# Turning gathered token tiles with VectorE's 32x32 transposes and sixteen small transfers in a routed-expert stage

## Chip, cores and metric

One core of a Trainium2 chip. The metric is the device time of one execution in microseconds; the program runs the whole layer once. Everything is float32.

## What is computed

One layer of a streaming encoder for 1024 tokens of width 1024: a gated DeltaNet branch and a sliding-window attention branch, added to the residual, and then a mixture of experts. Only the last part matters here:

```python
def hier_moe(h, ...):
    # top-1 of 4 groups, then top-2 of the 4 experts in it -> gates (tokens x 16)
    y = jnp.zeros_like(tok)
    for e in range(N_EXPERTS):                      # 16
        gu = tok @ w_gate_up[e]                     # 1024 -> 512
        act = jax.nn.silu(gu[:, :256]) * gu[:, 256:]
        y = y + gates[:, e:e + 1] * (act @ w_down[e])   # 256 -> 1024
```

`tok` is the RMS-normalised token row times `ffn_norm_g`, the gain that the kernel applies after it has turned the rows.

## The kernel before, in words

The front of the kernel (eight tiles of 128 tokens, 0 to about 660 us) writes the normalised rows to `h_mid` in HBM and the residual to `out`. Routing then gives each expert a list of token rows. An expert has one full tile of up to 128 rows, and up to two half tiles of 64 rows for what is over; a half tile that is empty is skipped by a branch on TensorE, which puts one small 64x64 transpose in its place (`nothing`, L827), while the other engines do their part for it always. Whatever doesn't fit goes through a spill loop.

The stage is a software pipeline over i = 0..15 (`ORDER` maps i to an expert), each engine with its own hand-written order:

- GpSimd gathers: `gather(i)` brings full tile i from `h_mid` into one of three buffers `hg[i % 3]`, `gather_half` the half tiles, `gather_base` the present rows of `out`; `scatter` writes the sum back. In iteration i it issues `gather(i + 3)` behind the gathers of the bases, and waits there until tile i has been turned.
- SyncE loads the weights, 2 MB (`load_gate_up`, L358) and 1 MB (`load_down`, L364) per expert, into a ring of four, so up to three experts ahead.
- TensorE, iteration i: `gate_up(i)` (8 steps of 128 rows, listed as 16 matmuls), `turn_glu(i-1)`, `turn_half_glu(i-1)`, `turn_halves(i)`, `down(i-1, 0)`, `down_half(i-1, 1)`, `gate_up_halves(i)`, `turn_rows(i+1)`, `down(i-1, 1)`, `down_half(i-1, 0)`. `turn_rows` is eight 128x128 transposes of the gathered rows into banks pm0 and pm1. The two halves of `down` use one bank, pm4, so the second waits until VectorE has added the first out (`y_ready`).
- VectorE, iteration i: `copy_half(i, 0/1)` (L1891), `add_out(i-1, 0)` (L1918), `add_half(i-1, 1)` (L1925), `copy_rows(i+1)` (L1825: two operations that copy the turned rows from PSUM to `hgT` times the gain), `add_out(i-1, 1)`, `add_half(i-1, 0)`, `swiglu(i)` (L1900, L1902), `half_swiglu(i, 0/1)` (L1909, L1911).
- ScalarE, iteration i: `gate_tanh(i)` (L1223), `copy_glu(i-1)` (L1229), `copy_half_glu(i-1, 0/1)` (L1236), `half_tanh(i, 0/1)` (L1243). It starts no transfer in this stage.

`gate_up(i+1)` needs `hgT`, which has one buffer: `copy_rows(i+1)` waits for `gate_up(i)` to end. `down(i-1, 0)` needs `copy_glu(i-1)`, which stands behind `gate_tanh(i)` in ScalarE's order. Matmuls and most transposes show as L423 and L426, the lines of the helpers `mm` and `turn`.

Of the kernel before, what the change touches and what calls it, by code (L numbers as in the profile page):

```python
# [70 lines left out]
def build(nc, x, x_turned, attn_norm_g, w_in, conv_w, a_log, dt_bias, out_norm_g, q_norm_g, k_norm_g, sinks,  # L71
          w_out, ffn_norm_g, b_group, b_expert, w_router, w_gate_up, w_down, out, dbg=None):
    with ExitStack() as ctx:
# [141 lines left out]
        hgT = flat(ctmp)[:, 0:D].rearrange("p (k n) -> p k n", n=P)  # L215
        hgT_half = [flat(ci)[:, c * 512:c * 512 + 512].rearrange("p (k n) -> p k n", n=P) for c in range(2)]
# [50 lines left out]
        M = sems("turned hT_ready gu_done tanh_ready glu_step glu_ready glu_turned glu_copied down_done y_ready", "slots_")  # L267
# [14 lines left out]
        def gated(i, c=0):  # L282

            return 3 * i + (3, 1, 2)[c] if i == NE - 1 else nth(i, c)

# [135 lines left out]
        def _(pe):  # L421
# [464 lines left out]
            def turn_glu(i):  # L886
                pe.wait_ge(M.glu_ready, gated(i))
# [22 lines left out]
            def turn_half_glu(i):  # L910
                pe.wait_ge(M.glu_ready, gated(i, 2))
                if_filled_both(i, pm[6:8], lambda c: None, lambda c: turn(pm[6 + c][:, 2 * P:3 * P], glu_half[c]), M.glu_turned)
# [82 lines left out]
        def _(act):  # L995
# [223 lines left out]
            def gate_tanh(i):  # L1219
                act.wait_ge(M.gu_done, gated(i))  # L1220
                if i:
                    act.wait_ge(M.glu_ready, gated(i - 1))
                act.activation(tnh, pm[2 + i % 2][:, 0:DE], ACT.Tanh, scale=0.5).then_inc(M.tanh_ready, 1)  # L1223

# [14 lines left out]
            def half_tanh(i, c):  # L1239
                act.wait_ge(M.gu_done, gated(i, c + 1))  # L1240
                if i:
                    act.wait_ge(M.glu_ready, gated(i - 1, c + 1))
# [3 lines left out]
            spilled = act.value_load(full[0:1, 0:1], min_val=0, max_val=2 ** (NE + 1) - 1)  # L1246
            for i in range(NE):
# [6 lines left out]
                for c in range(2):  # L1254
                    half_tanh(i, c)
            gate_tanh(NE - 1)
# [10 lines left out]
        def _(v):  # L1267
# [552 lines left out]
            def copy_rows(i):  # L1820
                v.wait_ge(M.turned, nth(i))
# [65 lines left out]
            def copy_half(i, c):  # L1887
                v.wait_ge(M.turned, nth(i, c + 1))
# [5 lines left out]

            def swiglu(i):
# [4 lines left out]
                v.scalar_tensor_tensor(tnh, tnh, 1.0, bank[:, 0:DE], ALU.add, ALU.mult).then_inc(M.glu_step, 1)  # L1900
                v.wait_ge(M.glu_step, gated(i))
                v.scalar_tensor_tensor(glu, tnh, 0.5, bank[:, DE:2 * DE], ALU.mult, ALU.mult).then_inc(M.glu_ready, 1)  # L1902

            def half_swiglu(i, c):
# [4 lines left out]
                v.scalar_tensor_tensor(t, t, 1.0, pm[6 + c][:, 0:P], ALU.add, ALU.mult).then_inc(M.glu_step, 1)  # L1909
                v.wait_ge(M.glu_step, gated(i, c + 1))  # L1910
# [17 lines left out]
            spilled = v.value_load(full[0:1, 0:1], min_val=0, max_val=2 ** (NE + 1) - 1)  # L1928
            for i in range(NE - 1):
# [10 lines left out]
                copy_rows(i + 1)  # L1940
# [5 lines left out]
                half_swiglu(i, 1)  # L1946
            last = NE - 1
# [23 lines left out]
        def _(g):  # L1971
# [123 lines left out]
            def gather(i):  # L2095
                if i >= IN:
                    g.wait_ge(gathered[i % IN], 16 * uses(i - IN, IN))
                    g.wait_ge(M.turned, nth(i - IN))
# [3 lines left out]
            def gather_half(i, c):  # L2102
                u = 2 * i + c
                if u >= HIN:
                    g.wait_ge(half_gathered[u % HIN], 16 * uses(u - HIN, HIN))
                    g.wait_ge(M.turned, nth(i - HIN // 2, c + 1))
# [44 lines left out]
            for i in range(NE + 1):  # L2151
                if i < NE:
# [3 lines left out]
                if i + IN < NE:  # L2156
                    gather(i + IN)
# [52 lines left out]
```

## Time and profile before

| | us |
|---|---|
| median of 3 runs | 948.48 (947.60 to 948.57) |
| the profiled execution | 949.3 |
| its span, first to last instruction | 947.5 |
| TensorE / VectorE / ScalarE / GpSimd busy | 900.2 / 586.8 / 230.7 / 217.4 |
| transfers over the span | 113.9 MB, 120 GB/s on average |

The page divides the span into forty slices of 23.7 us; a digit is the busy share in tenths, and PEclk the clock that TensorE was granted. The chain of work is followed back from the last instruction. In the lists in order of time a row gives the start, the time taken, engine, line, operation, output<-inputs, shape and count, and in brackets how long the engine had been idle before and what released it. Several operations of one kind that follow each other are merged into one row. "ACTq" and "SPq" are the instructions with which ScalarE and SyncE start transfers; they do not count as busy.

### The profile page before, as it was taken

To read this page: it belongs to the slowest core of one execution; us is meant where nothing else is said; L and a number is where in the kernel's file an instruction comes from. 1 tells how busy PE (TensorE), PEld (TensorE's weight loads), DVE (VectorE), ACT (ScalarE), POOL (GpSimd) and SP (SyncE) were. 2 spreads that over 40 slices of the span, in tenths; PEclk is the share of its full clock that TensorE was granted. 3 is DMA by queue.
4 is the path that set the end of the run, shared out by engine and by line. 5 is a ranking of instruction groups with operands and counts; after the bars stand their busy time and mean duration, and the time that the engine had idled before them with its cause. 6 is when DMAs were issued, how large, how long until landed. Compare 5 with 4: busy or idle time off the path is not lost.

```text
span 947.5 us, 16439 instructions
## 1 busy us (share of the span) xinstructions
PE 900.2 (95%) x6268; PEld 603.3 (64%) x6268; DVE 586.8 (62%) x1746; ACT 230.7 (24%) x637; POOL 217.4 (23%) x302
## 2 busy tenths in 40 slices
PE   5999899999999999999999999889899999999986
PEld 5687687696596787768769656565544554544532
DVE  2367776785785786687687577768344433544443
ACT  1343331431432332342243134123001001011000
POOL 7020020020020001002002000300444544555653
PEclk9999999999999999999999999999999999999998
DMA  8920101010010010110100004704559869899521
GB/s 307 395 112 1 45 24 45 15 55 23 24 67 12 35 68 1 46 46 23 46 23 2 29 18 144 278 24 142 178 163 338 282 212 313 292 324 345 183 87 43
DMA packets 50475, 113.86 MB, mean 120 GB/s; under 512 B 11207, under 2 KB 12487, under 8 KB 50384
## 3 DMA queue, kind: packets, MB, share of 16 engines
q1 hardware_dynamic: 34064, 87.07, 25.7%
q0 software_dynamic: 14592, 25.22, 7.8%
q8 instruction: 62, 1.02, 0.5%
q10 hardware_dynamic: 1728, 0.31, 0.2%
q14 instruction: 29, 0.24, 0.1%
HBM read 112.54 MB, written 25.17 MB: 145 GB/s over the span
## 4 chain that ended last, share of the span: by engine, by line
PE 86%; DVE 7%; DMA 2%; SPq 2%; issue 1%; POOL 0%; ACT 0%; POOLq 0%; DVEq 0%
PE pm L423 78%; PE pm L426 7%; DMA w_sb<-in_w_in 2%; DVE pqkv L1491 1%; SPq L351 1%; PE pm L827 1%; SPq L334 1%; DMA qkvT<-h_mid,w_sb 1%; DVE xT L1314 0%; DVE X L1673 0%; DVE bs L1735 0%; DVE ctmp L1825 0%; DVE sc L1659 0%; DVE aTm L1686 0%; DVE pT L1556 0%
## 5 line engine op out<-in xcount | busy, mean ns | idle before, releaser
L423 PEld LDWEIGHTS pm<-hT,w_sb 128*128 128x128 f32 x1544 | 176.4, 194 | 5.5 <-issue 2.9
L423 PE MATMUL pm<-hT,w_sb 128*128 128x128 f32 x1544 | 177.5, 277 | 1.9 <-DVE hT L1443 1.9
L423 PE MATMUL pm<-w_sb,hT 128*128 128x512 f32 (+1 forms) x384 | 153.4, 542 | 0.6 <-DMA w_sb<-in_w_in 0.6
L2030 POOL TENSOR_TENSOR tail<-tail,rows 128x512 f32<-128x512 f32 x8 | 10.8, 1346 | 485.9 <-ACT aTm L1046 485.9
L423 PE MATMUL pm<-wo_sb,pT 128*128 128x512 f32 x256 | 115.4, 597 | 2.7 <-ACT pT L1093 1.4
L423 PE MATMUL pm<-w_sb,ctmp 128*128 128x512 f32 (+1 forms) x264 | 102.7, 600 | 2.1 <-DVE ctmp L1825 2.1
L423 PEld LDWEIGHTS pm<-w_sb,hT 128*128 128x128 f32 x384 | 69.9, 193 | 52.2 <-issue 46.6
L1491 DVE SCALAR_TENSOR_TENSOR pqkv<-ci,cw,pqkv 128x128 f32<-128x128 f32 x288 | 77.4, 344 | 15.8 <-ACT pqkv L1025 15.6
L423 PEld LDWEIGHTS pm<-wo_sb,pT 128*128 128x128 f32 x256 | 46.6, 190 | 52.8 <-issue 48.8
L423 PEld LDWEIGHTS pm<-w_sb,ctmp 128*128 128x128 f32 (+1 forms) x264 | 39.9, 175 | 58.9 <-issue 58.5
L1891 DVE TENSOR_TENSOR ci<-pm,gain 128x512 f32<-128x512 f32 x32 | 20.6, 685 | 77.1 <-PE pm L426 38.7
L1673 DVE TENSOR_TENSOR X<-X,pm 128x256 f32<-128x256 f32 (+1 forms) x40 | 16.7, 418 | 54.3 <-PE pm L423 54.3
L423 PE MATMUL pm<-w_sb,Y 128*128 128x512 f32 x96 | 48.0, 623 | 2.4 <-issue 2.4
L1223 ACT ACTIVATE X<-pm 128x256 f32<-128x256 f32 x16 | 6.1, 384 | 163.3 <-PE pm L423 163.3
L1825 DVE TENSOR_TENSOR ctmp<-pm,gain 128x512 f32<-128x512 f32 x32 | 20.5, 683 | 31.3 <-PE pm L426 31.3
L2127 POOL DMA_INDIRECT pqkv<-out,w_sb x24 | 24.1, 1005 | 61.9 <-DMA out<-pqkv,w_sb 55.0
L423 PEld LDWEIGHTS pm<-X,aTm 64*64 64x64 f32 x640 | 23.2, 138 | 22.0 <-DVE X L1673 14.2
L423 PE MATMUL pm<-X,aTm 64*64 64x64 f32 x640 | 27.8, 227 | 8.0 <-DVE X L1673 6.9
L1012 ACT ACTIVATE ci<-pm 128x512 f32<-128x512 f32 x22 | 13.2, 601 | 90.2 <-PE pm L423 75.6
L1134 ACT ACTIVATE Y<-pm 128x256 f32<-128x256 f32 (+1 forms) x48 | 18.4, 384 | 68.6 <-PE pm L423 68.6
L1020 ACT ACTIVATE tail<-pm 128x512 f32<-128x512 f32 (+1 forms) x24 | 12.7, 528 | 88.4 <-PE pm L423 88.4
L1542 DVE TENSOR_TENSOR sc<-sc,pm 128x512 f32<-128x512 f32 x16 | 11.0, 685 | 36.7 <-PE pm L423 36.5
(340 smaller groups left out, 1456.6 us busy)
## 6 DMA issues: line engine op xcount, KB each, us to landing
w_sb<-in_w_gate_up SPq DMA_DIRECT2D x12, 2048.0 KB, 14.7
w_sb<-in_w_down SPq DMA_DIRECT2D x12, 1024.0 KB, 6.3
wo_sb<-in_w_gate_up SPq DMA_DIRECT2D x4, 2048.0 KB, 13.5
w_sb<-in_w_in SPq DMA_DIRECT2D x3, 2048.0 KB, 20.5
xt<-in_x SPq DMA_DIRECT2D x8, 512.0 KB, 4.3
xT<-in_x_turned SPq DMA_DIRECT2D x8, 512.0 KB, 3.6
w_sb<-in_w_in SPq DMA_DIRECT2D x4, 1024.0 KB, 13.4
wo_sb<-in_w_out SPq DMA_DIRECT2D x1, 4096.0 KB, 21.9
```

The source lines that it names most:

```text
L423: return pe.matmul(o_, lhsT=l_, rhs=r_, start=start, stop=stop, skip_group_check=True)
L426: return pe.transpose(o_, in_, ident[:, :])
L1012: ins = act.activation(ci[:, H * c:H * c + H, HALO:HALO + P], heads(pm[BANK[c]]), ACT.Copy)
L1020: act.activation(tail[:, c0 - 3 * HP:c0 - 3 * HP + n], pm[BANK[c]][:, 0:n], ACT.Copy).then_inc(F.chunk_copied, 1)
L1134: act.activation(Yd[rows_], heads(pm[3], CH)[rows_], ACT.Copy).then_inc(B.y_copied, 1)
L1491: ins = v.scalar_tensor_tensor(cv[:, i, :], ci[:, i, j:j + P], cw[:, j, i:i + 1], cv[:, i, :], ALU.mult, ALU.add)
L1542: v.tensor_tensor(xr[:, 512 * n:512 * n + 512], xr[:, 512 * n:512 * n + 512], late_banks(self.t)[n][:, :], ALU.add).then_inc(B.xm_ready, 1)
L1673: v.tensor_tensor(Xd[rows_], Xd[rows_], heads(pm[2], CH)[rows_], ALU.subtract).then_inc(B.x_updated, 1)
L1825: v.tensor_tensor(hgT[:, 4 * n:4 * n + 4, :], heads(pm[n]), wide(gain2[:, 4 * n:4 * n + 4]), ALU.mult).then_inc(M.hT_ready, 1)
L1891: v.tensor_tensor(hgT_half[c].rearrange("p k (d n) -> p k d n", d=2), heads(pm[c]).rearrange("p k (d n) -> p k d n", d=2), by_half, ALU.mu ...
L2030: g.tensor_tensor(qk_in[:, 0:QH, :], qk_in[:, 0:QH, :], gqk[:, None, 0:DH].broadcast_to([P, QH, DH]), ALU.mult)
L2127: g.indirect_dma_start(yo_half[u % HOUT], None, rows_of_out, slots_half(i, c), bounds_check=2 * T - 1, oob_is_err=False).then_inc(half_mov ...
```

## The change

For experts 1 to 15 the full tile is no longer turned by TensorE. VectorE transposes all 32x32 blocks of the gathered 128x1024 tile in one instruction into `blocks` (the room of `aTm`); this leaves block rows in the wrong quarter of the partitions. ScalarE then starts sixteen SBUF-to-SBUF transfers of 32 partitions x 256 elements (32 KB each), from quarter b to quarter a, into `moved` (the room of `pT`). VectorE applies the gain from there into `hgT` (`gain_rows`), with the same two operations of 512 elements. `turn_blocks(i+2)` stands at the end of VectorE's iteration i, `move_blocks(i+2)` at the end of ScalarE's. The first expert and the spill loop keep the old way. GpSimd issues `gather(i+3)` first in its iteration; `glu_step` is merged into `glu_ready`, which counts by two.

```diff
@@ TensorE
                 gate_up_halves(i)
-                turn_rows(i + 1)
                 if i:
                     down(i - 1, 1)
@@ ScalarE
+            def move_blocks(i):
+                act.wait_ge(M.blocks_turned, i)
+                if i > 1:
+                    act.wait_ge(M.hT_ready, rows_copied(i - 1))
+                for a in range(4):
+                    for b in range(4):
+                        to, of = [slice(QUARTER * n, QUARTER * n + QUARTER) for n in (a, b)]
+                        act.dma_start(moved[to, b * 256:b * 256 + 256], blocks[of, a * 256:a * 256 + 256]
+                                      ).then_inc(M.blocks_moved, 16)
...
+            move_blocks(1)
             for i in range(NE):
                 if i < NE - 1:
                     gate_tanh(i)
...
                 for c in range(2):
                     half_tanh(i, c)
+                if i + 2 < NE:
+                    move_blocks(i + 2)
@@ VectorE
+            def turn_blocks(i):
+                v.wait_ge(gathered[i % IN], 16 * uses(i, IN))
+                if i > 1:
+                    v.wait_ge(M.blocks_moved, 256 * (i - 1))
+                to = blocks.rearrange("p (a k n) -> p k a n", a=4, n=QUARTER)
+                v.transpose(to, hg[i % IN].rearrange("p (k a n) -> p k a n", a=4, n=QUARTER)).then_inc(M.blocks_turned, 1)
+
+            def gain_rows(i):
+                v.wait_ge(M.blocks_moved, 256 * i)
+                v.wait_ge(M.gu_done, gated(i - 1))
+                rows_ = moved.rearrange("p (b k n) -> p k b n", b=4, n=QUARTER)
+                for n in range(2):
+                    ks = slice(4 * n, 4 * n + 4)
+                    v.tensor_tensor(hgT[:, ks, :].rearrange("p k (b n) -> p k b n", b=4), rows_[:, ks],
+                                    gain2[:, ks].unsqueeze(2).unsqueeze(3).broadcast_to([P, 4, 4, QUARTER]),
+                                    ALU.mult).then_inc(M.hT_ready, 1)
...
+            turn_blocks(1)
             for i in range(NE - 1):
                 copy_half(i, 0)
...
-                copy_rows(i + 1)
+                gain_rows(i + 1)
...
                 half_swiglu(i, 1)
+                if i + 2 < NE:
+                    turn_blocks(i + 2)
@@ GpSimd
             for i in range(NE + 1):
+                if i + IN < NE:
+                    gather(i + IN)
                 if i < NE:
                     gather_base(i)
                     for c in range(2):
                         gather_base_half(i, c)
-                if i + IN < NE:
-                    gather(i + IN)
```

## Rows read from the trace of the kernel before

**Rows 1.** The page: busy us (share of the span) and instructions of each engine.
```profile
PE 900.2 (95%) x6268; PEld 603.3 (64%) x6268; DVE 586.8 (62%) x1746; ACT 230.7 (24%) x637; POOL 217.4 (23%) x302
```
**Rows 2.** Table of stretches: length, busy us per engine, clock, transfer share, GB/s.
```profile
722.51:735.47 12.96, 12.62 (x41) 5.81 (x39) 6.35 (x13) 1.44 (x6) 5.27 (x6) 1.00 0.96 328
...
883.35:902.14 18.79, 18.79 (x84) 9.06 (x83) 7.86 (x15) 1.45 (x6) 12.58 (x13) 1.00 0.49 156
```
**Rows 3.** In order of time, iteration 3 (no half tile filled); start us, duration us.
```profile
724.99 0.29 DVE L1911 SCALAR_TENSOR_TENSOR gsz<-X,pm 128x128 f32<-128x128 f32 x1
...
729.69 0.38 ACT L1223 ACTIVATE X<-pm 128x256 f32<-128x256 f32 x1 [11.23 <-PE pm L423]
...
730.13 1.29 DVE L1891 TENSOR_TENSOR ci<-pm,gain 128x512 f32<-128x512 f32 x2 [4.86 <-PE pm L827]
...
730.44 1.96 PE L423 MATMUL pm<-w_sb,Y 128*128 128x512 f32 x4 [0.34 <-issue]
...
732.52 0.75 DVE L1918 SCALAR_TENSOR_TENSOR hT<-pm,w_sb,hT 128x512 f32<-128x512 f32 x1 [1.10 <-PE pm L423]
...
733.49 1.88 PE L423 MATMUL pm<-w_sb,Y 128*128 128x512 f32 x4
```
**Rows 4.** The same view, iteration 1: the eight transposes and the product behind.
```profile
703.25 1.09 PE L426 MATMUL pm<-ident,y_mix 128*128 128x128 f32 x8
...
704.18 1.88 PE L423 MATMUL pm<-w_sb,Y 128*128 128x512 f32 x4
```
**Rows 5.** The same view, start of iteration 1: VectorE, and TensorE's first product.
```profile
686.74 0.19 DVE L1936 COPY w_sb<-pm 128x32 f32<-128x32 f32 x1 [4.03 <-PE pm L423]
687.66 1.29 DVE L1825 TENSOR_TENSOR ctmp<-pm,gain 128x512 f32<-128x512 f32 x2 [0.73 <-PE pm L426]
...
689.09 7.11 PE L423 MATMUL pm<-w_sb,ctmp 128*128 128x512 f32 x16 [1.47 <-DVE ctmp L1825]
```
**Rows 6.** Groups by line and shape on VectorE: busy us, mean ns.
```profile
L1686 DVE STREAM_TRANSPOSE aTm<-X 128x256 f32<-128x256 f32 x32 | 14.0, 439 | 0.3
...
L1290 DVE TENSOR_TENSOR bs<-bs 128x4 f32<-128x4 f32 x42 | 6.8, 162 | 1.4
```
**Rows 7.** Transfer starts in order of time: three of ScalarE's, SyncE's pair of iteration 3.
```profile
4.38 0.34 ACTq L1197 DMA_DIRECT2D cw<-in_conv_w  x1
...
7.87 0.57 ACTq L1197 DMA_DIRECT2D gain<-in_ffn_norm_g  x1
...
11.27 0.61 ACTq L1197 DMA_DIRECT2D w_rt<-in_w_router  x1
...
722.63 0.37 SPq L364 DMA_DIRECT2D w_sb<-in_w_down  x1
...
723.04 0.47 SPq L358 DMA_DIRECT2D w_sb<-in_w_gate_up  x1
```
**Rows 8.** In order of time: iterations 4 and 13, last glu step and down products.
```profile
738.42 0.29 DVE L1911 SCALAR_TENSOR_TENSOR gsz<-X,pm 128x128 f32<-128x128 f32 x1
...
743.86 1.88 PE L423 MATMUL pm<-wo_sb,Y 128*128 128x512 f32 x4
...
891.67 1.98 PE L423 MATMUL pm<-w_sb,Y 128*128 128x512 f32 x4
```
**Rows 9.** The last expert: TensorE in order of time, and one stretch as in rows 2.
```profile
918.58 0.44 PE L426 MATMUL pm<-ident,gsz 128*128 128x128 f32 x2 [1.53 <-DVE gsz L1902]
...
920.23 3.78 PE L423 MATMUL pm<-w_sb,Y 128*128 128x512 f32 x4
...
924.18 8.18 PE L423 MATMUL pm<-wo_sb,ctmp 128*128 128x512 f32 x16
...
920.00:921.00 1.00, 1.00 (x2) 0.61 (x3) 0.76 (x2) 0.45 (x2) 0.69 (x2) 0.50 0.17 53
```
**Rows 10.** Transfers by line: count, KB each where known, median us from start to landing.
```profile
h_mid<-y_mix SPq DMA_DIRECT2D x7, 512.0 KB, 2.6
...
XT_qkT<-h_mid,w_sb POOLq DMA_INDIRECT x16, 5.7
```

More of the change, by code:

```diff
@@ L215, in build @@
         hgT = flat(ctmp)[:, 0:D].rearrange("p (k n) -> p k n", n=P)
+        moved = flat(pT)
+        blocks = aTm[:, :, :, :].rearrange("p a h n -> p (a h n)")
         hgT_half = [flat(ci)[:, c * 512:c * 512 + 512].rearrange("p (k n) -> p k n", n=P) for c in range(2)]
@@ L265, in build @@
         A = sems("exp_in exp_out picks ranked rank_ready hots", "ahead_")
[L267 removed]
+        M = sems("blocks_turned blocks_moved turned hT_ready gu_done tanh_ready glu_ready glu_turned glu_copied down_done y_ready", "slots_")
         gathered = [ctx.enter_context(nc.semaphore(f"gathered{b}")) for b in range(IN)]
@@ L284, in gated, with halves_turned_by_pe, by_blocks @@
             return 3 * i + (3, 1, 2)[c] if i == NE - 1 else nth(i, c)
+        def halves_turned_by_pe(i, c):
+            return 2 * i + c + 2
+        def by_blocks(i):
+            return 0 < i < NE
         def rows_copied(i, c=0):
@@ L1820, in copy_rows @@
             def copy_rows(i):
-                v.wait_ge(M.turned, nth(i))
+                v.wait_ge(M.turned, 1 if i == 0 else NE + 2 + i)
                 if i:
@@ L1887, in copy_half @@
             def copy_half(i, c):
-                v.wait_ge(M.turned, nth(i, c + 1))
+                v.wait_ge(M.turned, halves_turned_by_pe(i, c))
                 if i:
@@ L1899, in swiglu @@
                     v.wait_ge(M.glu_turned, gated(i - 1))
-                v.scalar_tensor_tensor(tnh, tnh, 1.0, bank[:, 0:DE], ALU.add, ALU.mult).then_inc(M.glu_step, 1)
-                v.wait_ge(M.glu_step, gated(i))
+                v.scalar_tensor_tensor(tnh, tnh, 1.0, bank[:, 0:DE], ALU.add, ALU.mult).then_inc(M.glu_ready, 1)
+                v.wait_ge(M.glu_ready, 2 * gated(i) - 1)
                 v.scalar_tensor_tensor(glu, tnh, 0.5, bank[:, DE:2 * DE], ALU.mult, ALU.mult).then_inc(M.glu_ready, 1)
@@ L1908, in half_swiglu @@
                 t = tnh_half[c]
-                v.scalar_tensor_tensor(t, t, 1.0, pm[6 + c][:, 0:P], ALU.add, ALU.mult).then_inc(M.glu_step, 1)
-                v.wait_ge(M.glu_step, gated(i, c + 1))
+                v.scalar_tensor_tensor(t, t, 1.0, pm[6 + c][:, 0:P], ALU.add, ALU.mult).then_inc(M.glu_ready, 1)
+                v.wait_ge(M.glu_ready, 2 * gated(i, c + 1) - 1)
                 v.scalar_tensor_tensor(glu_half[c], t, 0.5, pm[6 + c][:, P:2 * P], ALU.mult, ALU.mult).then_inc(M.glu_ready, 1)
@@ L2097, in gather @@
                     g.wait_ge(gathered[i % IN], 16 * uses(i - IN, IN))
-                    g.wait_ge(M.turned, nth(i - IN))
+                    if by_blocks(i - IN):
+                        g.wait_ge(M.blocks_turned, i - IN)
+                    else:
+                        g.wait_ge(M.turned, 1 if i == IN else NE + 2 + i - IN)
                 g.indirect_dma_start(hg[i % IN], None, h_mid, slots(i),
@@ L2105, in gather_half @@
                     g.wait_ge(half_gathered[u % HIN], 16 * uses(u - HIN, HIN))
-                    g.wait_ge(M.turned, nth(i - HIN // 2, c + 1))
+                    g.wait_ge(M.turned, halves_turned_by_pe(i - HIN // 2, c))
                 g.indirect_dma_start(hg_half[u % HIN], None, rows_of_h, slots_half(i, c),
```

8 lines of the change are left out of this document (4 added, 4 removed).

## Prediction, made before the changed kernel was run

> **What bounds the kernel now.** I read the page first: TensorE is busy 95% of the span, ScalarE 24% [rows 1]. Only the routed-expert stage, from 670 us on, is touched. The table of stretches cuts it at the starts of the full tile's gate-up product (I call that start G_i for expert i): the iteration of 12.96 us from G_3 = 722.51 to G_4 = 735.47 holds 12.62 us of TensorE work, the one of 18.79 from G_13 = 883.35 holds 18.79, at full clock, while ScalarE works 1.4 us in each [rows 2]. So what leaves TensorE pays nearly in full unless it covers a wait, and ScalarE has over 11 us free per iteration. The question is where in the iteration these lie. The list in order of time shows it [rows 3]: ScalarE idles 11.23 us while TensorE works on the product, then gives the tanh (729.69) and right behind it the copy of the previous expert's turned glu, and 0.75 us after the tanh's start the down product begins (730.44). That copy is on TensorE's path with no slack: ScalarE may do other things from about G to G+7.2, and not a microsecond longer.
>
> **What the change removes.** Fifteen times (experts 1 to 15) eight 128x128 transposes leave TensorE. Start to start they hold 0.93 us (703.25 to 704.18) [rows 4]. But they stand between the two halves of the down product, which share one bank, and the second may start only when VectorE has added the first half out. Where no half tile's product lies between them, as in iteration 3, this wait is what comes late next: the add ends at 732.52 + 0.75 = 733.27 [rows 3]; with the 0.14 us that TensorE takes after VectorE (687.66 + 1.29 = 688.95, then 689.09 [rows 5]) the second half could start at 733.41 instead of 733.49. There the transposes are worth 0.08 us. With a half tile between, the whole 0.93 is saved. Of iterations 1 to 14 I count seven of each kind. In iteration 0, G_1 = 689.09 waits for the copy behind the transposes; without them VectorE can apply the gain from 686.74 + 0.19 = 686.93 on, for 1.28 us, and G_1 comes at 688.35, 0.7 earlier [rows 5]. Sum: 7 x 0.93 + 7 x 0.08 + 0.7 = 7.8 us.
>
> **What it adds on VectorE.** One 32x32 transpose of 128x1024 per expert, behind the last half-tile glu. The same operation on 128x256 takes 439 ns, and a small operation of this engine 162 ns [rows 6]; so 0.16 + 4 x 0.277 = 1.27 us, and not over 4 x 0.439 = 1.76. VectorE idles 4.86 us behind that place, until 730.13 [rows 3], which covers it; without that cover it would cost 14 x 1.27 = 18 us. The gain is read from SBUF instead of PSUM, two operations of the same size: I take the same time. If the strided read makes the pair 0.5 us slower, this reaches TensorE in the four shortest iterations only: 2 us for the range. The merged semaphore changes nothing. The gathers of full tiles go ahead of the bases and get two iterations (26 us and more) where they land in 5.7 [rows 2, 10]; nobody on TensorE's path waits for the bases moved behind them. Zero.
>
> **What it adds on ScalarE: the term that decides.** Per expert a wait for the transpose and sixteen transfer starts, between the half tiles' tanh of iteration i and the tanh of iteration i+1. Queued behind them stand the two instructions named above, and TensorE waits for the second. What does a start cost? The trace has no SBUF-to-SBUF transfer of 32 partitions. It has ScalarE's own starts at the beginning: 0.34 us for the first of a row, 0.57 for the eighth, seven intervals from 4.38 to 7.87, so 0.50 each. It has SyncE's pair in this very stage: 0.37, and the next 0.41 after it [rows 7]. Ends: 0.37 and 0.69 (the mean of ScalarE's ten intervals, 4.38 to 11.27). I take 0.455, midway between 0.41 and 0.50, because these too are starts in a row on a loaded chip: 16 x 0.455 = 7.3 us. They hold the instructions behind, since ScalarE's stream is taken in order.
>
> In time: in iteration 3, with a half tile's down product before G, the last glu step ends at 724.99 + 0.29 = 725.28, G+2.77; in iteration 4, without one, at 738.42 + 0.29 = G+3.24 [rows 3, 8]. Then come the transpose (1.2, its start overlaps), 0.1 for the signal, 7.3 of starts, and 0.75 from tanh to down product: G+12.1 or G+12.6. Now the down product starts at G+7.93 in the six iterations of the first sort (730.44), and between G+7.93 and G+8.39 (mean 8.18 over seven; the first is 743.86, the last 891.67) in the second [rows 3, 8]. Delay: 6 x 4.19 + 7 x 4.41 = 56.0 us. In iteration 1 one add fewer stands before the glu and the down product comes late anyway; I take 1.3 us less, 2.9. Sum 58.9 us, all on the path: TensorE has nothing else in its program there. Each 0.1 us per start is worth 16 x 14 x 0.1 = 22.4 us. Before iteration 0 the sixteen starts run beside the first gate-up product (7.1 us), and the tanh behind them is read only after the gain at 688.2: zero.
>
> **What the stalls do to TensorE's clock.** The trace shows such a stop once, in the last expert: a wait of 1.53 us and a shorter one follow the last product, and the granted clock goes to half (1.2 of 2.4 GHz; 0.50 in the stretch 920 to 921). Four matmuls then take 3.78 instead of 1.96 us and sixteen 8.18 instead of 7.13, in which it comes back: 2.87 us lost [rows 3, 8, 9]. The 1.47 us before G_1 left it at full: sixteen matmuls took 7.11 us [rows 5]. The new stops have about 4.2 us. I take one such loss per stall: 14 x 2.87 = 40.2 us. Bounds: 0 (it doesn't fall), and 14 x 3.84 = 54, if both down halves (1.96 and 1.88) run at half speed each time.
>
> The Trainium skill's page "TensorE: Matmul & The Clock Gate", section "HAM oscillation — how this bites in real kernels", tells of a loop whose transfer wait throttles the array anew in every tile. By it the loss is paid each time; our trace has a single case and can't say so.
>
> **The transfers themselves.** The last start ends at about G+11.4. 512 KB land 2.6 us after one start, gathers after 5.7 [rows 10]: G+14.0 to G+17.1. VectorE comes to the gain at G+12.1 + 2.08 (730.44 to 732.52) + 1.33 for two adds = G+15.5. So at most 1.6 us late, and this reaches TensorE only in the four shortest iterations: 0 to 6 us; I take 0. They add 0.5 MB to the 4.25 MB that such an iteration moves (12.96 us at 328 GB/s) on engines 0.96 busy [rows 2], but an iteration becomes 7 us longer, so the load per microsecond falls.
>
> **Sum.** The profiled execution took 949.3 us (span 947.5 and 1.8 around it). 949.3 - 7.8 + 58.9 + 40.2 = 1040.6; the median of the runs shown lies 0.8 lower: 1040 us.
>
> **The rivals.**
> 1. *The starts hold nobody up* (other side, faster). ScalarE is free in time if sixteen starts fit in 7.2 - 2.77 - 1.3 = 3.1 us, 0.19 each, or if its compute passes them by. Then only the saving is left: 949.3 - 7.8 - 0.8 = 941 us. Against it: the shortest start here is 0.34 on ScalarE and 0.37 on SyncE [rows 7]. For it: none of them moves as little as 32 rows. 7%.
> 2. *Stalls, but the clock stays up.* 949.3 - 7.8 + 58.9 - 0.8 = 1000 us; with starts of 0.37, which shorten the idle to under 3 us and make this likelier, 981. 16%.
> 3. *Starts are slower while the weights fill the queues.* ScalarE's mean of 0.69: 16 x 0.235 = 3.8 us more per iteration, 14 x 3.8 = 53: 1093 us. For it: the intervals on ScalarE grew after the eighth start; against: SyncE's pair in this stage kept 0.41. 13%.
> 4. *The change does less than it says*, and something takes the delay up, within 0.2%: 2%.
>
> The Trainium skill speaks for rival 1: "DMA: Bandwidth & Descriptors", section "Issuing engines are not separate DMA queues", calls the time to initiate a transfer "usually small relative to the DMA itself". The same page's "Rules for kernel authors" warns that transfers under 64 KB are mostly overhead, and these have 32 KB. Sixteen starts in a row side with the warning [rows 7].
>
> **How the numbers follow.** Forecast 62%, its own range 1015 to 1070 (starts of 0.41 to 0.50: -10 to +10; transpose up to +7; late blocks +6; clock loss 14 x 1.82, the four matmuls alone, to 14 x 3.84: -15 to +14). The range takes in rival 2's 1000 below and half-way cases to rival 3 above: 1000 to 1085 leaves out rival 1 (7%), the lower half of rival 2 (8%) and a good part of rival 3. A measurement of this kernel can tell about 0.2% from no change. Faster 7%, same 2%, slower 91%.
>
> **What would show it.** Right: sixteen starts of 0.4 to 0.5 us on ScalarE in each iteration; a TensorE stop of 4 us before each first down half, released by ScalarE's copy; the clock at half behind it; no eight transposes between the down halves except for the first expert. Wrong: starts of 0.2 us or less; a gain operation that waits for a transfer; the half tiles' copies on VectorE later than before relative to G. The prediction falls if ScalarE's compute goes on during the starts.

## The result: 14% slower, and the profile after

The changed kernel takes 1077.37 us (median of four, 1073.36 to 1079.82) against 948.04 for the kernel before beside it (942.02 to 948.57): a ratio of 1.138, 95% interval 1.132 to 1.143. The profiled execution took 1079.82 us with a span of 1078.0, against 949.3 and 947.5. Forecast was 1040, range 1000 to 1085: sign, mechanism and range held, the middle was 37 us too low.

The page of the changed kernel: engines (busy us, share of the span, instructions), the granted clock in 40 slices, the chain that ended last by engine, the groups that answer to the steps of the prediction (busy us, mean ns, then idle us before them and its releaser), and the new transfers (count, KB, median us to landing).

```profile
PE 922.9 (86%) x6148; PEld 600.8 (56%) x6148; DVE 603.0 (56%) x1761; ACT 230.5 (21%) x637; POOL 216.8 (20%) x302
...
PEclk9999999999999999999999999987789868878878
...
PE 76%; issue 10%; DVE 7%; DMA 2%; ACTq 2%; SPq 2%; POOL 0%; ACT 0%; DVEq 0%; POOLq 0%
...
L433 PE MATMUL pm<-w_sb,Y 128*128 128x512 f32 x96 | 73.5, 908 | 85.3 <-issue 76.5
...
L1232 ACT ACTIVATE X<-pm 128x256 f32<-128x256 f32 x16 | 6.1, 383 | 272.6 <-issue 250.3
...
pT<-aTm ACTq DMA_DIRECT2D x240, 32.0 KB, 5.7
```

Against [rows 1] TensorE has 120 instructions fewer (15 x 8 transposes) and yet is busy 22.7 us longer: the same down products at a lower clock. In the group of the down products with one kind of weight tile, 85 us of idle time have appeared. ScalarE is no busier, and yet its tanh is late: 250 us of the time before it count as "issue", time in which it waits for nothing that the profile shows. In 146 us of them (fourteen groups of starts, 10.2 to 11.1 us each) it is starting transfers; the page doesn't count that as busy.

Iteration 3 in order of time (start us, us, engine, line; "ACTq" are ScalarE's transfer starts; in brackets the idle time before and its releaser), against [rows 3]:

```profile
743.12 7.13 PE L433 MATMUL pm<-wo_sb,ctmp 128*128 128x512 f32 x16
...
745.60 0.29 DVE L1950 SCALAR_TENSOR_TENSOR gsz<-X,pm 128x128 f32<-128x128 f32 x1
745.80 1.24 DVE L1922 STREAM_TRANSPOSE aTm<-sc 128x1024 f32<-128x1024 f32 x1
747.07 10.22 ACTq L1241 DMA_DIRECT2D pT<-aTm  x16
...
757.39 0.38 ACT L1232 ACTIVATE X<-pm 128x256 f32<-128x256 f32 x1 [20.01 <-issue]
757.67 0.38 ACT L1248 ACTIVATE Y<-pm 128x256 f32<-128x256 f32 x1
...
758.15 3.75 PE L433 MATMUL pm<-w_sb,Y 128*128 128x512 f32 x4 [7.45 <-issue]
...
762.02 0.75 DVE L1957 SCALAR_TENSOR_TENSOR hT<-pm,w_sb,hT 128x512 f32<-128x512 f32 x1 [9.99 <-PE pm L433]
...
762.83 1.98 PE L433 MATMUL pm<-w_sb,Y 128*128 128x512 f32 x4 [0.69 <-DVE hT L1957]
763.35 1.28 DVE L1930 TENSOR_TENSOR ctmp<-pT,gain 128x512 f32<-128x512 f32 x2
```

The gate-up product ends at 750.25, and the tanh that reads it should run there. ScalarE is in the middle of its sixteen starts, which hold it from 747.07 to 757.29. The tanh comes 0.10 us behind the last of them, the copy behind the tanh, and the down product at G+15.03 instead of G+7.93. TensorE stands for 7.45 us, not the 4 us forecast. Behind it the first four products run at half clock (3.75 us against 1.96 [rows 3]), as the table of stretches shows with a granted clock of 0.51:

```profile
758.15:761.90 3.75, 3.75 (x5) 1.21 (x6) 0.00 (x0) 0.24 (x2) 0.06 (x1) 0.51 0.65 203
```

Everything else is as foretold: the turn takes 1.24 us (estimate 1.27) in VectorE's gap, the gain read from SBUF 1.28 (1.29 before), and it waits for no transfer here.

Start to start between the iterations' full-tile products, the 132.5 us that appear between G_0 and the last down half of iteration 14 divide as follows (each iteration of the changed kernel against the same one before):

| term | forecast | in the trace |
|---|---|---|
| first down half later relative to G, iterations 1 to 14 | +58.9 | +103.0 (6.3 to 8.1 each, median 7.3) |
| clock behind the stops | +40.2 | +36.8 (1.5 to 3.7 each) |
| transposes gone, iterations 1 to 14 | -7.1 | about -7.1 |
| G_1 relative to G_0 | -0.7 | +1.8 (17.36 against 15.52) |

That is 134.5, of which 1.9 of the last clock loss falls behind the stretch. The span grew by 130.5, since the changed kernel had 1.0 us less ahead of G_0, and behind the stretch the 1.9 stand against 2.9 less in the last expert, where the half clock of [rows 9] didn't come about.

The third row is the forecast itself and not a measurement: in the trace only the sum of the clock's loss and the saving is seen, and I have taken the saving as forecast. The experiments without transfers and with a busy TensorE, below, bear on it.

The start of iteration 1:

```profile
674.80 10.24 ACTq L1241 DMA_DIRECT2D pT<-aTm  x16
...
688.49 1.29 DVE L1930 TENSOR_TENSOR ctmp<-pT,gain 128x512 f32<-128x512 f32 x2 [2.56 <-DMA pT<-aTm]
...
689.93 8.80 PE L433 MATMUL pm<-w_sb,ctmp 128*128 128x512 f32 x16 [4.23 <-DVE ctmp L1930]
```

Sixteen starts of 7.3 us together would have ended at 682.1 and, if the last block lands 3.4 us behind them as it does here, the blocks would have been there at 685.5 (an estimate). They ended at 685.04, the gain waited 2.56 us for the last block, and the product behind a stop of 4.23 us ran below full clock (8.80 against 7.11 [rows 5]).

### The profile page after: what moved, and what is told of

Read it like the earlier page. It is cut to its first block, busy times and chain, and to the rows that moved or that the text cites. A ratio compares the mean times of both kernels' runs of the same rounds, so it can differ in the third digit from the quotient of the medians.

```text
span 1078.0 us, 16467 instructions
## 1 busy us (share of the span) xinstructions
PE 922.9 (86%) x6148; PEld 600.8 (56%) x6148; DVE 603.0 (56%) x1761; ACT 230.5 (21%) x637; POOL 216.8 (20%) x302
## 4 chain that ended last, share of the span: by engine, by line
PE 76%; issue 10%; DVE 7%; DMA 2%; ACTq 2%; SPq 2%; POOL 0%; ACT 0%; DVEq 0%; POOLq 0%
PE pm L433 70%; PE pm L436 5%; ACTq L1241 2%; DMA w_sb<-in_w_in 2%; DVE pqkv L1513 1%; SPq L361 1%; PE pm L837 1%; SPq L344 1%; DMA qkvT<-h_mid,w_sb 0%; DMA pT<-aTm 0%; DVE xT L1336 0%; DVE bs L1757 0%; DVE X L1695 0%; DVE sc L1681 0%; DVE aTm L1708 0%
## 5 line engine op out<-in xcount | busy, mean ns | idle before, releaser
L433 PE MATMUL pm<-w_sb,Y 128*128 128x512 f32 x96 | 73.5, 908 | 85.3 <-issue 76.5
L433 PE MATMUL pm<-w_sb,ctmp 128*128 128x512 f32 (+1 forms) x264 | 105.0, 610 | 4.8 <-DVE ctmp L1930 4.2
L433 PEld LDWEIGHTS pm<-w_sb,Y 128*128 128x128 f32 x96 | 23.7, 273 | 108.8 <-issue 102.7
L1957 DVE SCALAR_TENSOR_TENSOR tail<-pm,w_sb,tail 128x512 f32<-128x512 f32 x12 | 9.0, 751 | 68.3 <-PE pm L433 68.3
L1957 DVE SCALAR_TENSOR_TENSOR xt<-pm,w_sb,xt 128x512 f32<-128x512 f32 x10 | 7.5, 751 | 68.2 <-PE pm L433 68.2
L433 PE MATMUL pm<-wo_sb,Y 128*128 128x512 f32 x32 | 20.9, 793 | 21.6 <-issue 21.6
L433 PE MATMUL pm<-w_sb,ci 128*64 128x256 f32 x288 | 36.2, 411 | 0.0
```

The costliest lines, as they stand in the source:

```text
L433: return pe.matmul(o_, lhsT=l_, rhs=r_, start=start, stop=stop, skip_group_check=True)
L1957: v.scalar_tensor_tensor(y, down_bank(i, n)[:, :], gate, y, ALU.mult, ALU.add).then_inc(M.y_ready, 1)
```

## Why is a start 0.64 us and not 0.455?

The table of stretches, cut at three groups of sixteen starts (start:end, length; busy us of TensorE, its weight loads, VectorE, ScalarE, GpSimd; clock; share of the transfer engines; GB/s):

```profile
674.80:685.04 10.24, 10.24 (x58) 5.78 (x56) 1.55 (x3) 0.00 (x0) 0.99 (x1) 1.00 0.23 54
721.03:731.94 10.91, 3.74 (x13) 1.67 (x11) 1.29 (x2) 0.00 (x0) 4.85 (x5) 0.81 1.04 364
...
747.07:757.29 10.22, 3.63 (x12) 1.56 (x10) 1.29 (x2) 0.00 (x0) 4.92 (x6) 0.89 1.04 356
```

10.24 us at 54 GB/s and 10.22 at 356 GB/s: the pace doesn't follow the load. So rival 3 of the prediction ("slower while the weights fill the queues") has nearly its size and not its cause. What is left is the form of the transfer, the engine, or something of this place in the program. Two theories for the experiments:

- *S*: ScalarE's time in starts is the cause of the stop, its price is that of a start between two SBUF tiles, and it is nearly independent of bytes, partitions and load.
- Rivals: the transfers' traffic or late blocks cause the stop (*T*); the small pieces are what makes a start dear (*B*); the VectorE turn or its place costs (*V*).

## Experiments

**No transfers.** The gain reads the block buffer in place of the moved one, so the tiles from the second expert on hold blocks at the wrong partitions; the sixteen starts are left out and all the rest stays.

```diff
-            move_blocks(1)
...
-                if i + 2 < NE:
-                    move_blocks(i + 2)
...
-                rows_ = moved.rearrange(...)
+                rows_ = blocks.rearrange(...)
```

> The changed kernel without the sixteen transfers: VectorE's transpose stays, the gain reads the untransferred blocks, so the tiles are wrong and the rest of the work is the same. Theory A: what is left is the saving of the forecast, 7.8 us: seven iterations shorter by 0.93 us, seven by 0.08, and G_1 0.7 earlier: 941 us. Theory B (the transpose on VectorE or the new order costs something by itself): 948 us or more.

Measured: 942.09 us (941.67 to 942.82), ratio 0.983 (0.980 to 0.985) to its own kernel before, span 940.5, clock 0.992.

```profile
712.84 1.95 PE L433 MATMUL pm<-w_sb,Y 128*128 128x512 f32 x4 [0.24 <-issue]
...
715.72 1.98 PE L433 MATMUL pm<-w_sb,Y 128*128 128x512 f32 x4 [0.70 <-DVE xt L1945]
...
761.83 1.95 PE L433 MATMUL pm<-w_sb,Y 128*128 128x512 f32 x4 [1.48 <-issue]
```

The whole loss goes with the transfers; the turn and the gain from SBUF cost nothing, which ends *V*. 942 is what rival 1 had given (941). Where no half tile stands between, the down halves begin 2.88 us apart instead of 3.05: 0.17 saved, with VectorE's add now the visible wait, as the prediction had it (0.08). From G_0 (672.27) to the last down half of iteration 14 (907.50) it is 235.23 us against 239.56 in the kernel before: 4.3 saved in the trace, 7.2 if the two places are set aside where something else came late (1.6 at 761.83, 1.2 in iteration 13; what it was is not shown). So the forecast saving of 7.8 is about right in gross, and a part of it is given back. The ratio to its own reference says more than that, 1.7%, because beside these runs the kernel before took 958.55 us (957.72 to 961.44), 10 more than beside the changed kernel. So the match with rival 1's 941 is one in microseconds alone. The trace of such an execution wasn't taken, and where the 10 us lie stays open.

**Sixteen starts on SyncE**, behind the gate-up weights in its order, none on ScalarE.

```diff
+            def move_blocks(i):
+                sp.wait_ge(M.blocks_turned, i)
+                ...
+                        sp.dma_start(moved[to, b * 256:b * 256 + 256], blocks[of, a * 256:a * 256 + 256]
+                                      ).then_inc(M.blocks_moved, 16)
```

> The same sixteen starts, issued by SyncE between its weight loads instead of by ScalarE; everything else as in the changed kernel. Theory A (ScalarE's sequencer is held, so TensorE waits for the copy of the turned glu): the stop before each first down half goes back to the 0.2 to 0.4 us of before. What is late next is the gain: starts at 0.64 us each end at about G+14.4, land some 4 us later, so no iteration is shorter than about 19 us; the shorter ones grow by 1.5 to 5.5 us, 35 us in all, plus a clock loss of 2.9 us in some six of them, minus 7 saved: about 990 us (965 if SyncE's starts take 0.41). Theory B (the transfers themselves or VectorE are the load, whoever starts them): near 1075 us.

Measured: 1003.82 us (1002.75 to 1005.24), ratio 1.047 (1.045 to 1.050), span 1001.7, clock 0.962.

```profile
712.51 10.51 SPq L374 DMA_DIRECT2D pT<-aTm  x16
...
730.66 1.29 DVE L1934 TENSOR_TENSOR ctmp<-pT,gain 128x512 f32<-128x512 f32 x2 [10.67 <-DMA pT<-aTm]
...
732.05 9.98 PE L449 MATMUL pm<-wo_sb,ctmp 128*128 128x512 f32 x16 [8.82 <-issue]
...
752.35 10.07 PE L449 MATMUL pm<-w_sb,ctmp 128*128 128x512 f32 x16 [4.49 <-issue]
```

The stop ahead of the down half is gone (0.24 to 0.42 us before it), and another stands ahead of the gate-up product: the gain waits for blocks every time (1.4 to 10.7 us). SyncE started 3 MB of weights in the 4 us before these sixteen, and the gain could begin 7.6 us behind the last start (730.66 against 723.02), where the last block of the changed kernel landed 4.6 us behind it with the same weights under way (761.89 against 757.29). That the order in SyncE's queue makes this difference fits and is not shown. The time is 14 us over the 990 expected. The same transfers with the same bytes cost a third here (4.7% instead of 13.8), and at another place: so what stopped the down product is ScalarE's time, and *T* falls for that kernel. The pace is much the same on this engine, 10.51/16 = 0.66 us (0.68 over all its groups, ScalarE's 0.65); it isn't ScalarE's own.

**Half the transfers** on ScalarE (the even source quarters b; half of each tile is left unmoved).

```diff
                     for b in range(4):
+                        if not (b % 2 == 0):
+                            continue
```

> Only eight of the sixteen transfers (b = 0 and 2), the other half of the data is left where it was. Theory A, cost per start: ScalarE is held 8 x 0.64 = 5.1 us less, the stop before each down half falls from 7.4 to 2.3 us, 14 x 5.1 = 72 us less: 1005 us, and down to 975 if the shorter stop leaves the clock up. Theory B, cost from waiting for the landing or a fixed cost per expert: above 1040 us.

Measured: 987.71 us (984.36 to 991.06), ratio 1.030 (1.025 to 1.035), span 982.6, clock 0.976.

```profile
708.26 5.85 ACTq L1243 DMA_DIRECT2D pT<-aTm  x8
...
714.97 3.35 PE L433 MATMUL pm<-w_sb,Y 128*128 128x512 f32 x4 [2.96 <-issue]
...
889.65 1.95 PE L433 MATMUL pm<-w_sb,Y 128*128 128x512 f32 x4 [2.56 <-issue]
```

Eight starts take 5.0 to 5.9 us, and the stop is 1.1 to 3.0 us instead of 7: ScalarE's time less what was free. The time lies between the two figures expected, 1005 with the clock's loss and 975 without. Behind the two stops shown, of 2.96 and 2.56 us, the four products take 3.35 and 1.95: the clock falls at some of these shorter stops and not at others.

**A busy TensorE in the stop.** Eight products of constants (listed as 16 matmuls), into the down product's bank while it is free, ahead of each first down half; transfers as in the changed kernel.

```diff
+                    if i > 1:
+                        pe.wait_ge(M.y_ready, added(i - 2, RIGHT))
+                    keep_busy(pm[4], 8)
                     down(i - 1, 0)
```

> The changed kernel with eight dummy products (ident by ident, into the down product's bank before it is used; some 6.9 us at full clock) on TensorE inside each stop. Theory A with the clock term: the clock stays at full, the down halves go back to 1.96 us and the stops' aftermath (about 37 us in 14 iterations) goes: 1040 us. If the half clock cost nothing beyond the stop: 1077 us.

Measured: 1049.07 us (1048.85 to 1049.3), ratio 1.094 (1.091 to 1.097), span 1047.1, clock 0.988 instead of 0.928.

```profile
746.42 7.13 PE L433 MATMUL pm<-ident 128*128 128x512 f32 x16
...
754.12 1.96 PE L433 MATMUL pm<-w_sb,Y 128*128 128x512 f32 x4 [0.57 <-issue]
```

The products fill the stop but for at most 1.6 us, and the down half behind runs at full clock (1.96 in this row, 1.88 to 1.96 in all fourteen). The start of the down product isn't any earlier; only the loss of clock is taken away. It is worth 28 us by the medians, 31 by the spans, and 41 by the ratios (1.138 - 1.094), since the two kernels ran in sets in which the kernel before differs by 10 us. The 36.8 of the trace lie within. This trace also measures what the table above had to take over from the forecast. From G_0 (673.38) to the last down half of iteration 14 (1014.43) it takes 341.05 us against 372.02, with its first down halves 2.5 us later in sum. So the clock's loss is 33.4 us in the stretch and 35.3 with the 1.9 behind it, not 36.8; and the saving, at full clock, is 5.8 us, not 7.1.

**The price of a start by its form.** Behind the changed kernel's work, six groups of eight starts on ScalarE, each awaited: 32x256 between SBUF tiles in the same quarter, in another quarter, 32x64, 128x256; then 32x256 and 128x256 from HBM.

```diff
+            starts("f_same", [(into[q[n % 4], n * 256:n * 256 + 256], blocks[q[n % 4], 0:256]) for n in range(8)])
...
+            starts("f_loads", [(into[q[n % 4], n * 256:n * 256 + 256], h_mid[n * 32:n * 32 + 32, 0:256]) for n in range(8)])
```

> The changed kernel with six groups of eight more starts on ScalarE behind all work: 32x256 within a quarter, 32x256 between quarters, 32x64 between quarters, 128x256, 32x256 from HBM, 128x256 from HBM. The last start intervals tell what sets the 0.64 us. Theory 'per start': all six groups near 0.64. Theory 'SBUF on both sides': 0.64 for the first four, 0.4 to 0.5 for the HBM ones. Theory 'bytes': the 32x64 group is shorter and the 128-partition ones longer. Time of the whole: some 1110 us, of no meaning.

Measured (one run, 1111.55 us):

```profile
1071.30 24.83 ACTq L1292 DMA_DIRECT2D w_sb<-aTm  x32
1097.67 8.80 ACTq L1292 DMA_DIRECT2D w_sb<-h_mid  x16
```

The first row joins the four groups between SBUF tiles, waits between them included, the second the two from HBM. Within the groups the starts follow each other every 0.64 us in all four SBUF forms (0.61 us for the instruction; 0.65 and 0.62 with 128 partitions, and one interval of 1.51 in the first group) and every 0.47 to 0.48 from HBM (0.44 to 0.46); the first of a group takes 0.51 to 0.53 and 0.35. So 8 KB or 128 KB, 32 or 128 partitions, the same quarter or another make no difference of more than 0.01, and this at a time at which nothing else moves: *B* falls. Two SBUF ends cost 0.17 us more per start than one; no run shows why.

**The kernel before again.** Unchanged.

> The kernel before, unchanged, for a profile on the same chip as the others. If the 10 us by which it ran longer beside the last comparison belong to the chip, its profile here shows them again in one place: the stretch from 665 to 690 us, the iterations, or the front. Near 948 or near 958 us.

Measured: 944.96 us (942.68 to 947.93, eight executions), beside 946.35 (942.28 to 950.94, 29), ratio 0.999 (0.996 to 1.001). Its trace has a span of 941.6, and from G_0 to the last down half of iteration 14 it takes 239.56 us, just as the first trace. The rest of the difference is 2.9 us ahead of G_0 and 3.0 in the last expert:

```profile
917.25 1.99 PE L423 MATMUL pm<-w_sb,Y 128*128 128x512 f32 x4
...
919.34 7.13 PE L423 MATMUL pm<-wo_sb,ctmp 128*128 128x512 f32 x16
```

3.78 and 8.18 there in [rows 9]. The single half-clock case on which I had built the clock's price doesn't come in every execution of the same kernel.

**Starts shared out.** Eight on ScalarE, eight on SyncE ahead of its weights, VectorE's turn right behind the gain (some 4 us earlier in the iteration). All sixteen blocks are moved. The edit of VectorE alone is shown:

```diff
                 gain_rows(i + 1)
+                if i + 2 < NE:
+                    turn_blocks(i + 2)
```

> Right output, the same sixteen transfers: eight started by ScalarE, eight by SyncE ahead of its weight loads, and VectorE's transpose put directly behind the gain, 3 us earlier. Theory A: ScalarE is held from about G+1.2 to G+6.4 and free before the tanh at G+7.2, so the stop before the down half goes away; the blocks land by G+9 to G+12 and the gain is due at G+11.5 in the shortest iterations: 942 to 950 us. If the cost were in the transfers (queues, landing), the gain would wait 3 us or more in every iteration: above 980.

Measured: 948.93 us (945.51 to 951.54, twelve), ratio 1.0025 (1.0005 to 1.0044) to 946.35.

```profile
720.12 5.35 ACTq L1261 DMA_DIRECT2D pT<-aTm  x8
...
734.35 1.29 DVE L1950 TENSOR_TENSOR ctmp<-pT,gain 128x512 f32<-128x512 f32 x2 [2.03 <-DMA pT<-aTm]
...
735.75 7.11 PE L451 MATMUL pm<-w_sb,ctmp 128*128 128x512 f32 x16 [1.87 <-issue]
```

No stop is left ahead of the down halves: of 13.8% of loss 0.25 is left, with nothing taken out of the work. What its trace shows of the distance to the 942 us of the kernel with no transfers is the landing: in nine iterations the gain waits for a block (22.8 us together, 3.4 at most), and in four it reaches TensorE for 1.0 to 3.3 us (735.75, 838.24, 854.45, 870.94); behind two of these the gate-up product also runs below full clock (8.80 us against 7.11).

**The same, and the second down half in a bank of its own**, so that it needn't wait for VectorE's add.

```diff
-            return pm[1 - n] if i == NE - 1 else pm[4]
+            return pm[1 - n] if i == NE - 1 else pm[(4, 0)[n]]
```

> As split, and the second down half goes to bank pm0, which the tiles no longer need, so it does not wait for VectorE's add. The 0.69 to 0.88 us that seven iterations wait between the down halves go: 5 to 6 us under split, if the gain is not the later of the two; no change against split if the gain sets the end in those iterations.

Measured: 948.16 us (945.49 to 952.93, twelve), ratio 1.002 (0.9995 to 1.004): no different from the one above. The time won between the halves turns up ahead of the gate-up product, where the gain still waits for blocks (28.7 us in ten iterations, 5.2 at most) and four stops of 1.3 to 4.4 us stand.

**Fewer starts, by way of HBM.** One store of the block buffer to HBM and four loads back, one for each quarter, on ScalarE at the place of the sixteen.

```diff
+                act.dma_start(through, blocks[:, 0:D]).then_inc(M.blocks_moved, 16)
+                act.wait_ge(M.blocks_moved, 80 * (i - 1) + 16)
                 for a in range(4):
-                    for b in range(4):
-                        ...
+                    act.dma_start(moved[QUARTER * a:QUARTER * a + QUARTER, :].rearrange("n (b x) -> n b x", b=4),
+                                  through[:, a * 256:a * 256 + 256].rearrange("(b n) x -> n b x", b=4)
+                                  ).then_inc(M.blocks_moved, 16)
```

> The sixteen transfers are replaced by one store of the whole block buffer to HBM (128x1024) and four loads back, one for each quarter, all started by ScalarE at the same place in its order; it waits for the store to land before it starts the loads. Theory (the cost is what one start takes times their number, 0.64 us between SBUF tiles and 0.47 where HBM is one side): 0.5 for the store, some 2.6 for its landing and 4 x 0.47 = 1.9, so ScalarE is held about 5.0 us from each turn. With eight transfers it was held 5.3 to 5.9 and TensorE stopped for 2.5 to 3.0 before the down product; here 2.1, and nothing of the clock at most of them: 942 + 14 x 2.1 = 971, 965 to 985, about 1.03 of the kernel before. Rival (what holds ScalarE is the wait for its transfers' data or the whole transfer of 0.5 MB, whatever the form): a stop like that of the changed kernel, 1040 or more.

Measured: 1056.8 us (1051.37 to 1059.67), ratio 1.104 (1.101 to 1.108), span 1049.6: a miss by 86 us.

```profile
740.06 0.34 ACTq L1240 DMA_DIRECT2D through<-aTm  x1
748.75 1.89 ACTq L1243 DMA_DIRECT2D pT<-through  x4
750.74 0.38 ACT L1233 ACTIVATE X<-pm 128x256 f32<-128x256 f32 x1 [19.08 <-issue]
...
751.50 3.56 PE L434 MATMUL pm<-w_sb,Y 128*128 128x512 f32 x4 [8.12 <-issue]
```

The starts cost what was said: 0.34 for the store and 1.76 to 2.11 for four loads, 2.2 us in place of 10.2. But the store, 512 KB as in [rows 10], doesn't land in 2.6 us: ScalarE waits for it from 740.40 to 748.75, and in the first twelve iterations from 690 on the loads start 7.1 to 8.7 us behind the store's start (5.1 and 3.9 in the last two). The stops of 5.5 to 8.1 us in these twelve (3.7 and 2.8 in the last two) are near the changed kernel's 7 because ScalarE is held nearly as long, 8.9 to 10.6 us, and what holds it is another thing.

**The same, with VectorE's turn right behind the gain.**

> The same store and four loads, and VectorE turns the next tile right behind the gain of this one instead of behind the gating, some 4 us earlier in the iteration. ScalarE is then held for about 5 us in a stretch in which it waits for the gate-up product anyway (its tanh comes 7.1 us after that product's start). Theory: no stop before the down product and none before the gate-up product, clock full, so the time of the kernel with no transfer at all, which stood 6 to 8 us under a kernel before with the same front: 0.985 to 0.995 of the kernel before. Rival (turning early delays the next tile, because the gather of that tile has not landed, or the round through HBM lands late as the blocks on SyncE did): waits of 1 to 3 us before the gain in many iterations, 1.00 to 1.02.

Measured: 998.38 us (995.89 to 1003.7, six), ratio 1.043 (1.039 to 1.046), span 1001.1.

```profile
708.97 0.34 ACTq L1240 DMA_DIRECT2D through<-aTm  x1
711.62 2.53 ACTq L1243 DMA_DIRECT2D pT<-through  x4
...
748.69 0.34 ACTq L1240 DMA_DIRECT2D through<-aTm  x1
757.90 1.76 ACTq L1243 DMA_DIRECT2D pT<-through  x4
...
760.52 3.58 PE L434 MATMUL pm<-wo_sb,Y 128*128 128x512 f32 x4 [4.40 <-issue]
```

A miss again, and past the rival's range too, for the same reason: the store has landed 2.7 us after its start in some iterations (708.97) and 9.2 in others (748.69), and where it is late the tanh is late too, or the gain (35.8 us of waiting for loads, 8.3 at most, and once a stop of 8.11 us ahead of the gate-up product). Which iterations these are goes with what else moves, as stretches from the store's start to the first load's show (the last two numbers: share of the transfer engines, GB/s, the store included):

```profile
708.97:711.62 2.65, 2.65 (x11) 0.92 (x8) 1.53 (x3) 0.00 (x0) 1.01 (x1) 1.00 0.49 198
748.69:757.90 9.21, 7.43 (x26) 3.56 (x24) 4.27 (x10) 0.00 (x0) 5.06 (x5) 1.00 0.94 330
873.74:883.18 9.44, 6.47 (x19) 2.74 (x17) 4.27 (x10) 0.00 (x0) 5.05 (x5) 1.00 0.94 340
955.73:958.49 2.76, 2.76 (x10) 0.87 (x10) 0.75 (x1) 0.00 (x0) 0.00 (x0) 1.00 0.48 193
```

2.65 us at 198 GB/s are 0.52 MB, the store and nothing else; 9.21 us at 330 are 3.0 MB. The two kernels with a store have thirty such stretches. In the six in which under 0.1 MB of anything else moved, none with a weight load started in the 18 us before, it took 2.6 to 3.3 us; in the 21 in which over 1.3 MB moved, 6.2 to 9.4; the three between took 3.9 to 5.1. So the store is slow where other transfers are under way. That these are the weights, and not the gathers as well, no run separates.

**The changed kernel with only the turn moved** right behind the gain, all sixteen starts on ScalarE.

> The changed kernel with its sixteen transfers between SBUF tiles as they are, VectorE's turn alone moved to right behind the gain. Theory: ScalarE is held for 10.2 us from about the start of the gate-up product instead of 4 us behind it, so the tanh comes some 3.2 us late instead of 7.2: stops of about 3 us, as with half the transfers at the old place, 942 + 14 x 3.2 = 987 and up to 15 more where the clock falls: 985 to 1003, about 1.05. Rival (the starts are slowed by what else moves at the time or the stop has another cause than their sum): above 1030, near the changed kernel.

Measured: 1002.31 us (1001.58 to 1004.53), ratio 1.047 (1.044 to 1.051), span 1000.0, within the forecast 985 to 1003.

```profile
727.94 11.66 ACTq L1241 DMA_DIRECT2D pT<-aTm  x16
...
740.46 3.45 PE L433 MATMUL pm<-w_sb,Y 128*128 128x512 f32 x4 [5.96 <-issue]
...
864.30 1.95 PE L433 MATMUL pm<-w_sb,Y 128*128 128x512 f32 x4 [2.40 <-issue]
```

Nothing is taken from the starts (10.3 to 11.7 us for sixteen), they only begin between 4 us before G and 1 us behind it instead of 4 us behind it, and the stops shrink to 0.2 to 6.0 us (0.2, as in the kernel before, where the starts began at 792.52: from G-3.6 they ended at G+7.0). Two lines of order are worth 75 us by the medians, 86 by the ratios: what the starts cost is what of them lies beyond G+7.2.

## Why the prediction was right, and where it was off

- **What bounds the kernel, and the free stretch of ScalarE**: right. The stop stands ahead of the first down half in all fourteen iterations; moving the starts to another engine, halving them or beginning them earlier shrank it each time. In iteration 3 the down product came at G+15.03 where the forecast had G+12.1, and the 2.9 us between are the dearer starts (10.22 against 7.3). The page gives "issue" as what ended the stop, not ScalarE's copy as foretold, but the copy ends just ahead of the product (757.67 + 0.38, then 758.15).
- **The term that was mis-sized is the price of a start.** It said 0.455 us, midway between SyncE's 0.41 and ScalarE's 0.50 [rows 7], all of them starts with one end in HBM. The trace shows 10.22/16 = 0.64 in the iterations. 16 x (0.64 - 0.455) = 3.0 us per iteration, 14 x 3.0 = 41 of the 44 us by which the term came out larger (103 against 58.9). The prediction had said that it had no row of a transfer between SBUF tiles and bounded the price at 0.69; the value lay near that end. Rival 3 was priced by that end and gave 1093. The forecast's own range, 1015 to 1070, was missed by this term; 1077 lies in the stated range because that had been widened toward rival 3. Two of its signs of being right came with other numbers, starts of 0.64 us where it said 0.4 to 0.5 and stops of 7 where it said 4, and one of its signs of being wrong was seen, once: ahead of G_1 the gain waited for a transfer.
- **The remaining 3 us** are 0.2 per iteration, since some groups of sixteen took longer than 10.2 (10.91 from 721.03). Iteration 1, given 2.9 us, took 6.3; 3.0 of the difference are the dearer starts again.
- **The clock**: the loss comes in every stop, as forecast. Fourteen times the first four products took 3.34 to 3.75 us. 36.8 us in the trace (35.3 by the one with a busy TensorE) against 40.2; with TensorE kept busy the loss is gone. The case it was built on was a weak witness, though: it is missing in another execution of the same kernel. The Trainium skill's page "TensorE: Matmul & The Clock Gate", section "HAM oscillation — how this bites in real kernels", says of a loop whose transfer wait stops TensorE that it pays in every tile; this trace agrees for stops of about 7 us, with 14 of 14, while behind the shorter ones of the kernel with half the transfers the clock stayed up in some.
- **The saving**: without the transfers 7.2 us in gross (forecast 7.8), 4.3 net. The first part of it, G_1 0.7 earlier, holds in that kernel (14.70 us behind G_0 against 15.52), but in the changed kernel the sign turns: the prediction called the sixteen starts ahead of iteration 0 free, because only the tanh behind them was asked about, and not the last block that the gain itself waits for. That cost 1.8 + 0.7 = 2.5 us. By the estimate above the blocks would have been there at 685.5, before the gain could run (685.74 + 0.19), had a start taken 0.455: the omission was real, but at its own price it would have cost nothing.
- **VectorE's turn, the gain from SBUF, the merged semaphore, the load on the queues**: costed at nothing and found at nothing (1.24 and 1.28 us, hidden). The first three are also in the kernel with no transfers, whose loss is gone; they were not taken away one by one.
- **The Trainium skill's** "DMA: Bandwidth & Descriptors" calls the time to initiate a transfer "usually small relative to the DMA itself". Here a single one took 5.7 us to land and 0.64 to start, and the sixteen took 10.2 us to start: the sentence holds for one transfer and not for a group on one engine. "Rules for kernel authors" on the same page warns that transfers under 64 KB are mostly overhead. It points the same way, toward fewer of them, but here the size did not set the price: a start took 0.64 us for 8 and 32 KB and 0.65 for 128.
- **In sum**: +44.1 for the starts, -3.4 for the clock, +2.5 at G_1, -1.0 ahead of G_0 and -2.9 in the last expert make 39.3, from the forecast's 1040.6 to the profiled 1079.8. The last two are differences between executions, as large as those between two of the kernel before (2.9 and 3.0), and no merit or fault of the forecast. The medians differ by 37, because the profiled execution of the changed kernel lies 2.4 us above its median, not 0.8.

## What to carry to other kernels

An engine that looks three quarters idle isn't free: find out where within the iteration its gap lies and when its next instruction is wanted, then add up every transfer start as time on that engine, with the price of that form (0.64 us between SBUF tiles here), before anything of the data's own time. If the work must stay, move it to the start of the gap or share it out over two engines before shrinking it: two moved lines gave 75 us here and sharing out the starts the rest, while fewer starts with a landing to wait for gained little, from 1.138 to 1.104 at the old place and from 1.047 to 1.043 at the early one. And don't wait on an engine for a transfer that shares its path with megabytes of weights by the landing time that it had when the path was free.

## What the runs showed of the hardware that I had not expected

- A start between two SBUF tiles takes 0.64 us back to back on ScalarE and 0.66 on SyncE, for 8 KB as for 128 KB, at 54 as at 356 GB/s; from HBM it takes 0.47. The first of a group is shorter (0.51 and 0.35), so a lone start isn't a price for a series.
- The same store of 512 KB lands in 2.6 to 3.3 us where nothing else moves and in 6.2 to 9.4 beside over 1.3 MB of other transfers, in the same kernel.
- How long a stop of TensorE was doesn't settle whether the clock falls: behind 2.96 us four products took 3.35, behind 2.56 they took 1.95; behind 1.87 sixteen took 7.11, and in the same kernel behind 1.86 they took 8.80:

```profile
870.94 8.80 PE L451 MATMUL pm<-w_sb,ctmp 128*128 128x512 f32 x16 [1.86 <-issue]
```

- The unchanged kernel took 942 to 951 us in two sets of runs, the one beside the changed kernel and another, and 954 to 961 in the other two, on other chips; no trace shows why. Differences in microseconds between kernels of different sets are uncertain by as much.

No version that moves all the blocks beat the kernel before. The kernel with no transfers marks 942 us as the floor of this idea, 0.5 to 0.6% under the kernel before of the faster two sets and 1.7% under that of its own.
